# Wide feed-forward layers: all up units first, then down, with six of sixteen down units as seven products of summed blocks

## The reference

```python
D_FF_2 = 4 * D_MODEL      # 4096

def sqrelu_mlp(h, w_up, w_down):
    a = jnp.maximum(h @ w_up, 0)
    return (a * a) @ w_down

for i in range(DEPTH_2):                       # 4 layers
    ...                                        # y: attention of one of three kinds
    h = h + y
    h = h + sqrelu_mlp(rms_norm(h, mlp_norm_g[i]), mlp_w_up[i], mlp_w_down[i])
return rms_norm(h, final_norm_g)
```

## Time and profile before

| what | value |
|---|---|
| median of three runs | 2392.44 us |
| lowest and highest of them | 2390.06 and 2392.48 us |
| the profiled execution | 2390.82 us |
| its span in the trace, first to last instruction | 2389.0 us |
| TensorE busy | 2363.2 us, 99% |
| VectorE busy | 1724.2 us, 72% |
| ScalarE busy | 1453.1 us, 61% |
| GpSimd busy | 80.2 us, 3% |
| mean granted TensorE clock | 0.999 of full speed |

### The profile page before, as it was taken

How to read it: one execution, slowest core, us unless ns; L and a number is a source line. 1 busy time by engine, 2 the same in 40 slices (tenths; PEclk the granted TensorE clock), 3 DMA queues, 4 the chain that set the end, 5 groups by cost and what they waited for, 6 DMA issues and landing times. The chain is left out here.

```text
span 2389.0 us, 31585 instructions
## 1 busy us (share of the span) xinstructions
PE 2363.2 (99%) x12354; PEld 1993.6 (83%) x12354; DVE 1724.2 (72%) x1921; ACT 1453.1 (61%) x1674; POOL 80.2 (3%) x114
## 2 busy tenths in 40 slices
PE   9999999999999999999999999999999999999998
PEld 7889978788888888888878788888888888887887
DVE  5665466898898899889986766666666766668565
ACT  6454454688888888888856544454444544456442
POOL 0000010000000000000001100000000000003000
PEclk9999999999999999999999999999999999999999
DMA  8255552699999999999955355443555255553552
GB/s 313 94 196 209 184 209 73 255 372 357 352 364 356 347 363 370 346 356 373 359 204 201 132 209 187 178 176 117 207 189 192 88 192 190 188 189 124 188 192 105
DMA packets 81806, 555.18 MB, mean 232 GB/s; under 512 B 11072, under 2 KB 11840, under 8 KB 16192
## 3 DMA queue, kind: packets, MB, share of 16 engines
q1 hardware_dynamic: 81600, 552.19, 61.7%
HBM read 551.10 MB, written 1.05 MB: 231 GB/s over the span
## 5 line engine op out<-in xcount | busy, mean ns | idle before, releaser
L2159 DVE TENSOR_TENSOR wlo<-raw,whi 128x2048 fp32r<-128x2048 f32 x484 | 1106.2, 2296 | 427.8 <-ACT whi L1698 426.8
L1698 ACT ACTIVATE whi<-raw 128x2048 fp32r<-128x2048 f32 x487 | 931.7, 1928 | 512.2 <-PE bank L896 138.1
L818 PE MATMUL bank<-whi,xt 128*128 128x512 f32 (+1 forms) x1056 | 311.0, 379 | 2.9 <-DVE xt L2176 1.3
L1245 PE MATMUL bank<-whi,xt 128*128 128x512 f32 (+1 forms) x768 | 222.5, 374 | 1.6 <-DVE e_hf L2805 1.4
L818 PEld LDWEIGHTS bank<-whi,xt 128*128 128x128 f32 x1056 | 189.4, 188 | 40.3 <-issue 3.3
L818 PE MATMUL bank<-wlo,xt 128*128 128x512 f32 (+1 forms) x528 | 197.5, 374 | 0.0
L896 PE MATMUL bank<-whi,h_hi 128*128 128x512 f32 x596 | 184.3, 390 | 0.0
L896 PE MATMUL bank<-whi,h_lo 128*128 128x512 f32 x596 | 183.6, 389 | 0.0
L896 PE MATMUL bank<-wlo,h_hi 128*128 128x512 f32 x596 | 183.5, 389 | 0.0
L1062 PE MATMUL bank<-xt,whi 128*128 128x512 f32 x768 | 182.5, 390 | 0.0
L1062 PEld LDWEIGHTS bank<-xt,whi 128*128 128x128 f32 x768 | 142.7, 188 | 28.6
(11 more groups left out here) (346 smaller groups left out, 3676.5 us busy)
## 6 DMA issues: line engine op xcount, KB each, us to landing
raw<-in_units SPq DMA_DIRECT2D x509, 1024.0 KB, 5.0
gain<-in_ln_g SPq DMA_DIRECT2D x4, 512.0 KB, 6.8
gain<-in_ln_b SPq DMA_DIRECT2D x4, 512.0 KB, 8.4
gain<-in_attn_norm_g SPq DMA_DIRECT2D x4, 512.0 KB, 5.9
gain<-in_mlp_norm_g SPq DMA_DIRECT2D x4, 512.0 KB, 6.1
toep<-in_toeplitz SPq DMA_DIRECT2D x2, 768.0 KB, 9.5
cst<-in_cst SPq DMA_DIRECT2D x1, 1120.0 KB, 18.9
x<-in_x SPq DMA_DIRECT2D x4, 256.0 KB, 6.1
```

The lines of the kernel that those rows point to most:

```text
L818: mm = pe.matmul(proj_bank(l, c, t)[:, 0:width], a[:, kx, t * P:(t + 1) * P], b[:, k, :], start=(kx == 0 and i == 0), stop=(kx == KT - 1 a ...
L1245: mm = pe.matmul(bank[b][:, 0:width], a[:, kx, :], w[:, k, :], start=(kx == 0 and i == 0), stop=(kx == KT - 1 and i == 2))
L1698: act.activation(whi[u % NH][:, :], raw[u % NR][:, :], ACT.Copy).then_inc(hi_ready[u % NR], 2)
L2159: dve.tensor_tensor(wlo[u % NR][:, :], raw[u % NR][:, :], whi[u % NH][:, :].bitcast(F32), ALU.subtract).then_inc(lo_ready[u % NR], 2)
```

## The change

In the four wide layers the order and part of the arithmetic of the feed-forward part change:

- All up units run first, with banks 4 to 7 and 0 to 3 in turn for even and odd groups. Then come twelve down units in the order `FOLDS`, then `fold_last` as before with groups 6 and 7.
- Every second unit of `FOLDS` is a sum unit, six a layer (groups 2, 3 and 4). Its product of a 256 x 256 hidden block (2 token tiles x 2 row blocks) with a 256 x 1024 weight block (2 x 2 blocks of 512 columns) is made with Winograd's form of Strassen's scheme: 7 block products instead of 8, from sums of blocks. Each is still three matmuls.
- GpSimd forms the sums of hidden blocks and of weight blocks (`block_sums`): four small instructions for each of the groups 2 to 4, and for each sum unit one over 1024 and two over 512 columns, each of which needs the one before.
- ScalarE copies these sums to rounded high parts (`high_of_sums`), VectorE subtracts to get the low parts (`low_of_sums`): `op_lo` of 1024 columns, the unit's own low part in 512 and 1024 columns (one of its four blocks is in no product by itself), and the low part of the four sums, 2048 columns, last.
- Four of the seven products gather in banks 0 to 3 over all six sum units and are added by VectorE to `x` after the folds (`add_products`). The other three go straight to banks 4, 5 and 6.
- The two sets of buffers for the sums are used in turn. The first is `y` with `t_hi0` and `t_lo0`; the second lies in the place of the layer's transposed input `xt`, so it is free once the last up unit has been used.

```diff
+NSUM = 6
+FOLDS = [(0, 0), (2, 0), (0, 1), (2, 1), (1, 0), (3, 0), (1, 1), (3, 1), (5, 0), (4, 0), (5, 1), (4, 1)]
+LAST_FOLDS = [(6, 0), (6, 1), (7, 0), (7, 1)]
...
+A11, A21, A12, A22, S1, S2, S3, S4 = range(8)
+T1, T3, T2, T4 = range(4)
...
-                    if g:
+                    if g and k == HYB:
                         down[g - 1] = self.take(ws[g - 1] // 256)
+                if k != HYB:
+                    for g, j in FOLDS + LAST_FOLDS:
+                        down.setdefault(g, []).extend(self.take(1))
             self.gate.append(gate)
...
+SUM_UNITS = {l: [PLAN.down[l][g][j] for g, j in FOLDS[1::2]] for l in range(NL) if KIND[l] != HYB}
...
+            sum_f = [y[:, :, :].rearrange("p t d -> p (t d)"), t_f1[:, :]]
+            sum_high = [t_hi0[:, :], xt_lo.rearrange("p k s -> p (k s)")]
+            sum_low = [t_lo0[:, :], xt_hi.rearrange("p k s -> p (k s)")]
+            op_hi = [op_hi0[:, :], op_hi1[:, :]]
...
+            def block_sums(l):
+
+                hb = GRP0[l] - NAT[KIND[l]]
+                for g in range(2, 5):
+                    pool.wait_ge(h_mid, hb + g + 1)
+                    a = op_f[:, 2 * g - 4:2 * g - 2].rearrange("p u (n s) -> p u n s", s=P)
+                    pool.tensor_tensor(a[:, :, S3], a[:, :, A11], a[:, :, A21], ALU.subtract)
+                    link(pool.tensor_tensor(a[:, :, S1], a[:, :, A21], a[:, :, A22], ALU.add))
+                    link(pool.tensor_tensor(a[:, :, S2], a[:, :, S1], a[:, :, A11], ALU.subtract))
+                    pool.tensor_tensor(a[:, :, S4], a[:, :, A12], a[:, :, S2], ALU.subtract).then_inc(sums_ready, 1)
+                for i, u in enumerate(SUM_UNITS[l]):
+                    if i == 0:
+                        pool.wait_ge(turned, 4 * (3 * l + 2) + 4)
+                    elif i == 1:
+                        wait_used(pool, PLAN.up[l][7][-1])
+                    else:
+                        wait_used(pool, SUM_UNITS[l][i - 2])
+                    pool.wait_ge(loaded[u % NR], u // NR * 16 + 16)
+                    b = raw[u % NR][:, :].rearrange("p (k h c) -> p k h c", k=2, h=2)
+                    t = sum_f[i % 2].rearrange("p (n c) -> p n c", n=4)
+                    link(pool.tensor_tensor(t[:, T1:T3 + 1], b[:, :, 1], b[:, 0], ALU.subtract))
+                    link(pool.tensor_tensor(t[:, T2], b[:, 1, 1], t[:, T1], ALU.subtract))
+                    pool.tensor_tensor(t[:, T4], b[:, 1, 0], t[:, T2], ALU.subtract).then_inc(sums_ready, 1)
+
             for l in range(NL):
                 if KIND[l] != HYB:
...
+            def fold_plain(l, g, j, first):
+
+                a_hi, a_lo = hidden(l, g)
+                u = PLAN.down[l][g][j]
+                for t in range(NT):
+                    for kk in range(2):
+                        mm = fold_rows(u, a_hi, a_lo, 2 * j + kk, kk, t, first and kk == 0, False)
+                mm.then_inc(used[u % NR], 1)
...
+            def fold_sums(l, i):
+
+                u = SUM_UNITS[l][i]
+                b_hi, b_lo = (w[u % n][:, :].rearrange("p (k h c) -> p k h c", k=2, h=2)
+                              for w, n in ((whi, NH), (wlo, NR)))
+                t_hi, t_lo = (t[i % 2].rearrange("p (n c) -> p n c", n=4) for t in (sum_high, sum_low))
+                split_ready(u, 1)
+                for at, a, (b, c) in ((0, A11, (b_hi[:, 0, 0], b_lo[:, 0, 0])), (1, S1, (t_hi[:, T1], t_lo[:, T1])),
+                                      (2, S2, (t_hi[:, T2], t_lo[:, T2])), (3, S3, (t_hi[:, T3], t_lo[:, T3])),
+                                      (4, A12, (b_hi[:, 1, 0], b_lo[:, 1, 0])), (5, S4, (b_hi[:, 1, 1], b_lo[:, 1, 1])),
+                                      (6, A22, (t_hi[:, T4], t_lo[:, T4]))):
+                    high, low = (h[:, a * P:(a + 1) * P] for h in (op_hi[i % 2], op_lo[:, i]))
+                    for n, (v, w) in enumerate(((high, b), (low, b), (high, c))):
+                        mm = pe.matmul(bank[at][:, :], v, w, start=at < 4 and i == 0 and n == 0,
+                                       stop=at < 4 and i == NSUM - 1 and n == 2)
+                mm.then_inc(used[u % NR], 1)
+
...
-                    pe.wait_ge(nat_lo, n0 + 2)
-                    fold(PLAN.down[l][0], 0, True, second_group)
-                    for g in range(2, n):
-                        if g >= 3:
-                            pe.wait_ge(h_mid, hb + g)
-                        rise_wide(PLAN.up[l][g], g, n0 + 4)
-                        if 2 < g < n - 1:
-                            pe.wait_ge(hl_ready, hb + g)
-                        if g < n - 1:
-                            fold(PLAN.down[l][g - 1], g - 1, False)
+                    rise_wide(PLAN.up[l][2], rise_bank(l, 2), second_group)
+                    pe.wait_ge(nat_lo, n0 + 4)
+                    for g in range(3, n):
+                        if g >= 4:
+                            pe.wait_ge(h_mid, hb + g - 1)
+                        rise_wide(PLAN.up[l][g], rise_bank(l, g))
+                    pe.wait_ge(h_mid, hb + n - 1)
+                    for p, (g, j) in enumerate(FOLDS):
+                        if p % 2:
+                            if p == 1:
+                                pe.wait_ge(h_mid, hb + n)
+                            fold_sums(l, p // 2)
+                        else:
+                            if p == 8:
+                                pe.wait_ge(hl_ready, hl_at(l, 5))
+                            fold_plain(l, g, j, p == 0)
                 fold_last(l)
...
+            def high_of_sums(l, i):
+
+                if i == 1:
+                    wait_used(act, PLAN.up[l][7][-1])
+                    act.wait_ge(h_mid, GRP0[l] - NAT[KIND[l]] + 8)
+                elif i:
+                    wait_used(act, SUM_UNITS[l][i - 2])
+                act.wait_ge(sums_ready, SUMS0[l] + 3)
+                act.activation(op_hi[i % 2], op_f[:, i], ACT.Copy).then_inc(sums_hi, 1)
+                act.wait_ge(sums_ready, SUMS0[l] + 4 + i)
+                act.activation(sum_high[i % 2], sum_f[i % 2], ACT.Copy).then_inc(sums_hi, 1)
...
+                for p, (g, j) in enumerate(FOLDS):
+                    after([PLAN.down[l][g][j]])
+                    if p % 2 == 0 and p // 2 + 1 < NSUM:
+                        high_of_sums(l, p // 2 + 1)
...
+            def low_of_sums(l, i):
+
+                u = SUM_UNITS[l][i]
+                dve.wait_ge(sums_hi, 2 * (SUM0[l] + i) + 1)
+                dve.tensor_tensor(op_lo[:, i], op_f[:, i], op_hi[i % 2].bitcast(F32), ALU.subtract)
+                dve.wait_ge(hi_ready[u % NR], u // NR * 2 + 2)
+                dve.wait_ge(sums_ready, SUMS0[l] + 4 + i)
+                for h in (slice(0, 512), slice(1024, 2048)):
+                    dve.tensor_tensor(wlo[u % NR][:, h], raw[u % NR][:, h], whi[u % NH][:, h].bitcast(F32),
+                                      ALU.subtract)
+                dve.wait_ge(sums_hi, 2 * (SUM0[l] + i) + 2)
+                dve.tensor_tensor(sum_low[i % 2], sum_f[i % 2], sum_high[i % 2].bitcast(F32),
+                                  ALU.subtract).then_inc(lo_ready[u % NR], 2)
+
+            def add_products(l):
+
+                wait_used(dve, SUM_UNITS[l][-1])
+                blocks = x[:, :, :].rearrange("p t (h c) -> p (t h) c", h=2)
+                for i, at in enumerate((slice(0, 4), slice(1, 4), slice(2, 4), slice(1, 4, 2))):
+                    out = blocks[:, at]
+                    b = bank[(0, 2, 3, 1)[i]][:, :].rearrange("p c -> p () c").broadcast_to([P, (4, 3, 2, 2)[i], 512])
+                    link(dve.tensor_tensor(out, out, b, ALU.add))
 
...
+                for p, (g, j) in enumerate(FOLDS):
+                    after([PLAN.down[l][g][j]])
+                    if p % 2 == 0 and p // 2 + 1 < NSUM:
+                        low_of_sums(l, p // 2 + 1)
+                    if p in (7, 9):
+                        g = 6 if p == 7 else 7
+                        dve.wait_ge(hh_ready, hl_at(l, g))
+                        dve.tensor_tensor(h_lo[:, g % 2], (h_f, h_last)[g - 6][:, :], h_hi[:, g % 2].bitcast(F32),
...
+                add_products(l)
```

More of the change, by code:

```diff
@@ L119, in __init__ @@
                 s0 = STEP0[l]
-                for g in range(len(ws) + 1):
+                for g in range(len(ws) + (k == HYB)):
                     if g < len(ws):
@@ L914, in fold_by_halves, with hidden, fold @@
                 return mm
-            def hidden(g):
+            def hidden(l, g):
+                if KIND[l] != HYB and g == 5:
+                    return [h[:, :].rearrange("p (f s) -> p f s", s=S) for h in (h5_hi, h5_lo)]
                 return [h[:, g % 2].rearrange("p (f s) -> p f s", s=S) for h in (h_hi, h_lo)]
-            def fold(units, g, first, between=None):
-                a_hi, a_lo = hidden(g)
+            def fold_plain(l, g, j, first):
[20 more added lines that the diff above has]
+                mm.then_inc(used[u % NR], 1)
+            def fold(l, units, g, first):
```

(25 more changed lines are left out.)

96 lines of the change are left out of this document (75 added, 21 removed).

## The result

| | before | after |
|---|---|---|
| median (runs) | 2392.25 us (4) | 2424.68 us (4) |
| lowest to highest | 2390.06 to 2392.48 | 2423.13 to 2425.4 |
| the profiled execution: time, span | 2390.8, 2389.0 us | 2424.04, 2422.1 us |
| its mean granted clock | 0.999 | 0.991 |

After is slower: 1.0137 times before, 95% interval 1.0121 to 1.0153, or 32.4 us. The forecast was +14.5 us and 2407 us. The direction is right and the size is not.

What follows compares the result with a forecast made beforehand. TensorE was taken to bound the kernel, busy for 2363.2 of 2389.0 us. Per layer -4.08 + 7.70 = +3.62 us, four layers +14.5; 2390.8 + 14.5 + 1.6 = 2407 us, range 2384 to 2430.

Steps and rivals of the forecast that it cites:

- What the change removes: TensorE's sum units in the four wide layers take 21 matmuls instead of 24: 16.3 us, 4.08 us a layer.
- The order of the stages costs nothing: In the wide layers, running all ups first costs nothing by itself.
- What it adds: Per pair of folds: ScalarE 6.8 us, VectorE 7.7 us, GpSimd 4.9 us, against TensorE's 10.20 us.
- The added products at the end: VectorE's adds to x after the folds, at most 7.5 us, hidden with 2.5 us to spare.
- The collision: GpSimd and VectorE take turns, 11.8 us a pair against TensorE's 10.2; waits of 3.85 us at folds 3 and 7.
- The sum: Wide layers: -4.08 + 7.70 = +3.62 us each, +14.5 us in four, giving 2407 us.
- The prediction's own sign of being wrong: A granted TensorE clock below 1.00 after the waits would show the forecast wrong.
- the waits cost more than themselves: Rival, 20%: TensorE's clock falls in 8 waits, at most 38 us, 2445; half, or longer GpSimd instructions, 2416 to 2430.
- the forecast's own 2396 to 2415: TensorE waits of 5 to 9 us a layer give this time; 55%.
- The rival's ceiling of 4.76 us a fold: At the lower clock, the fold behind a wait takes TensorE up to 4.76 us more.
- the turns fall better: Rival, 13%: in the folds, waits fall below 4.08 us a layer, giving 2380 to 2397 us.
- the walk: GpSimd's and VectorE's shared queue followed through the folds: fold 3 starts at 19.5 us, third GpSimd sum before the low part.

Runs made afterwards that it cites:

- Experiment 2: Changed kernel with GpSimd's weight-block sums cut to two columns, other data split instead, their small place 512 bytes a partition: 2374.74 us, ratio 0.9928.
- experiment 5: Changed kernel's order of work without its arithmetic: all ups first, downs in the changed order, no sum units: 2391.35 us, ratio 0.9995 to before.
- experiment 1: Changed kernel with GpSimd's weight-block sums cut to two columns, other data split instead, their small place 32 bytes a partition: 2396.67 us, ratio 1.0019.
- experiment 7: Changed kernel with GpSimd's sums of a weight unit started only after VectorE's low parts of the previous unit's sums: 2415.37 us, ratio 1.0095.
- experiment 8: Changed kernel with the sums of weight blocks formed by VectorE instead of GpSimd: 2406.62 us, ratio 1.0062.
- 10: Changed kernel with four sum units a wide layer instead of six, at folds 1, 4, 7 and 10: 2381.24 us, ratio 0.9948.
- experiment 3: Changed kernel with 16 matmuls of zeros ahead of folds 3 and 7 of each wide layer: 2409.00 us, ratio 1.0069.
- experiment 4: Changed kernel with 8 matmuls of zeros ahead of folds 3 and 7 of each wide layer: 2415.68 us, ratio 1.0093.

## Why the prediction was off

- **What the change removes**, 16.3 us: right. Experiment 2 is the kernel with this term alone left, 4.09 us a layer.
- **The order of the stages costs nothing**: right, experiment 5.
- **What it adds**: right. ScalarE's and VectorE's additions are hidden by themselves (experiment 2). GpSimd's set taken at 4.9 us is 2.41 + 1.29 + 1.29 = 4.99 us where nothing is in the way. The added products at the end make no wait: TensorE's list of waits has none for them.
- **The collision**: right, in mechanism, place and size. I had waits of 3.85 us at folds 3 and 7, 7.7 a layer; these folds begin 3.87 us late, and they are 27.15 us apart (1461.42 to 1488.57), 24.3 without the clock's 2.86 in the first, where I had 24.2. The 2048 low parts are in two clusters, 2.28 and 3.35 us (4.6 was the upper end), and GpSimd's 512s reach 3.23. Each experiment that takes this work away or moves it (1, 2, 7, 8, 10) takes away or moves the waits. The Trainium skill's rule ("SBUF — State Buffer", section "SBUF: two separate sides"), that the pair of ports is held for a whole instruction and not shared in part, agrees with rows of after too: 1.81 us of VectorE's become 5.12 while GpSimd's sums run.
- **The sum**: this is the step that failed. It priced a wait at its own length, -4.08 + 7.70 a layer, with the clock at nothing. The clock fell in or behind all eight waits and took 18.2 us by the profile, 15.7 by experiment 3. The forecast would have been 2407 + 18 = 2425, which is the measured 2424.7. The prediction's own sign of being wrong, a granted clock below 1.00 after the waits, is what the profile shows. The price stood in the rival "the waits cost more than themselves", at most 38 us, with half of it as its middle, and its part of 20% was too low. It is also only through this rival that the range, up to 2430, takes in the measured time; the forecast's own 2396 to 2415 does not. The rival's ceiling of 4.76 us a fold was somewhat high as well: at the lower level matmuls start 0.43 us apart (1462.44, 1462.87 and 1463.29 us in layer 2), not twice 0.2267, so a whole fold at that level would take about 4.2 us more (an estimate, 21 x 0.20). The only row I had for it showed a low clock where TensorE ran dry, and waits of 3.85 us were in my own forecast; the two belonged together. The Trainium skill's page "TensorE: Matmul & The Clock Gate", section "Part 1: The HAM clock gate (the "warmup" mystery)", says that an idle TensorE falls to half its clock; I had left it out of the sum since this trace had no wait long enough to show it, and the trace of after shows it eight times of eight.
- The rival **"the turns fall better"** (2380 to 2397) needed the low part of sums ahead of GpSimd's third. It did not happen: the third (1457.08, 2.13 us) went ahead of the low part (1458.01, 3.35 us), as in the walk.

What stays open: why equal waits cost the clock in some places and not in others. Of waits of 1.9 us it was 2 of 8 in experiment 4 and 3 of 7 in experiment 8; in experiment 7 it was 4 of 16 waits of 0.3 to 2.6 us, and one of the two longest, 2.59 us in layer 3, cost nothing. The attention of layers 2 and 5 has a wait of 1.14 or 1.15 us in every kernel here; it cost the clock once each in the profiles of experiments 1, 3 and 4 and in no other. So the length of a wait alone doesn't decide, and why the same 3.7 us cost 1.7 us in two layers and up to 2.9 in two others isn't shown either.

## What to carry to other kernels

Where matmuls are bought with work on another engine, add up the time of everything that takes turns on the same path, here GpSimd and VectorE with two inputs from SBUF, and compare it with TensorE's time per step; one sum unit in three folds won 11 us, one in two lost 32. The comparison alone isn't enough when the two are nearly even: with 10.28 us of VectorE for 10.20 of TensorE experiment 8 still had three waits a layer of 1.5 to 1.9 us. Price a wait of TensorE at its length plus the clock's fall behind it, here 1.7 to 2.9 us for a wait of 3.7 us, and 1.6 us or nothing for one of 1.9. Where a wait can't be avoided, cut it: matmuls that need less go first, and lateness that cost 12.3 us a layer with the clock (7.7 + 4.6) costs 6.5.

## What the runs showed of the hardware

- A tensor of 32 bytes a partition made matmuls of 128 x 512 start 0.2333 us apart instead of 0.2267, 3%; with 512 bytes it was gone (experiments 1 and 2, 2396.67 and 2374.74 us). The slow ones are those whose hidden operand (the second name behind the arrow) was allocated behind the small tensor: all in the folds, all in the experts' down products (line 1443, a mean of 396 ns against 390), and half of those in the experts' up products. In these last the weights come from the same buffers and only the hidden operand's place differs; `xt` is allocated ahead of the small tensor, `odd_hi` and `odd_lo` behind it. TensorE in experiment 1:
```profile
508.64 0.39 PE L1362 MATMUL bank<-wlo,xt 128*128 128x512 f32 x1
...
509.32 0.39 PE L1362 MATMUL bank<-wlo,xt 128*128 128x512 f32 x1
...
709.33 0.40 PE L1362 MATMUL bank<-wlo,odd_hi 128*128 128x512 f32 x1
...
710.03 0.40 PE L1362 MATMUL bank<-wlo,odd_hi 128*128 128x512 f32 x1
```
Three matmuls take 0.68 us with `xt` and 0.70 with `odd_hi`. The wide layers' ups kept their 7.28 us for 32 such matmuls; both of their operands, `xt` and `whi`, are allocated ahead. So the place of the hidden operand is enough to make a matmul slower. Which addresses do so wasn't tried. Its cost, 22 us, is larger than the change's whole saving.
- GpSimd's sum of two inputs took 2.41 us for 1024 columns and 1.29 for 512, VectorE's 1.22 and 0.69.
- Matmuls of zeros hold the clock: with 16 of them in each wait it was 1.00 in all eight folds behind (experiment 3).
